# Output projection kept in PSUM under the feed-forward, first up product by token tiles, fewer semaphore clears: layers 2 and 3 of a three-layer block

## The reference

```python
x = x + mixer(rmsnorm(x, norm_mix)) @ w_out          # the output projection
h = rmsnorm(x, norm_ffn)
x = x + (silu(h @ w_gate) * (h @ w_up)) @ w_down     # D_FF = 2816 hidden columns
```

## Time and profile before

| | us |
|---|---|
| timed runs: median of 3 (lowest, highest) | 1140.2 (1139.49, 1145.4) |
| profiled execution, first to last instruction (span) | 1135.1 |
| PE busy in it | 998.4 |
| layer 2, output stage, from its first DMA | 568.08 |
| layer 3, output stage, from its first DMA | 921.86 |
| feed-forward of layer 3, up(0) begins | 952.39 |

### The profile page before, as it was taken

The page is one execution under the profiler, slowest core; times in us unless marked ns, Lnnn a source line. Parts: engine busy times, 40 slices in busy tenths (PEclk is TensorE's granted clock), DMA queues, the critical chain, the costliest instruction groups (busy, mean ns, idle before and its releaser), DMA issues. The chain is left out here.

```text
span 1135.1 us, 20168 instructions
## 1 busy us (share of the span) xinstructions
PE 998.4 (88%) x8497; PEld 710.3 (63%) x8499; DVE 590.4 (52%) x950; ACT 486.3 (43%) x795; POOL 101.3 (9%) x111
## 2 busy tenths in 40 slices
PE   6998899799666677998799999997998879999996
PEld 5675787455333344886547777775885536777773
DVE  5566589421000004688666555435667865555543
ACT  5456452310000004545556455524545656645532
POOL 3410360000000001033000000002040000000000
PEclk9899899799888898998889999998998999999999
DMA  9822005999999996452094755525422046666520
GB/s 273 247 90 82 2 3 226 422 409 420 421 421 421 421 411 195 155 177 76 1 329 133 243 193 184 183 105 153 149 82 75 1 174 216 223 222 204 188 89 37
DMA packets 108324, 228.56 MB, mean 201 GB/s; under 512 B 7145, under 2 KB 86043, under 8 KB 93659
## 3 DMA queue, kind: packets, MB, share of 16 engines
q1 hardware_dynamic: 105275, 219.38, 53.2%
q0 software_dynamic: 2976, 8.14, 2.5%
HBM read 224.63 MB, written 1.05 MB: 199 GB/s over the span
## 5 line engine op out<-in xcount | busy, mean ns | idle before, releaser
L524 DVE SCALAR_TENSOR_TENSOR ffn_wu_lo<-ffn_w_up,ffn_wu_hi 128x2048 f16<-128x2048 f32 x44 | 99.0, 2288 | 55.2 <-ACT ffn_wu_hi L449 55.2
L1132 PE MATMUL rw_pB<-ring,kept 128*32 128x256 f32 x864 | 69.2, 418 | 31.4 <-DMA ring<-in_w_up 22.0
L669 PE MATMUL ffn_pG<-ffn_hT_hi,ffn_wu_hi 128*128 128x256 f16 x352 | 96.0, 273 | 0.3
L669 PE MATMUL ffn_pG<-ffn_hT_lo,ffn_wu_hi 128*128 128x256 f16 x352 | 96.0, 273 | 0.0
L669 PE MATMUL ffn_pG<-ffn_hT_hi,ffn_wu_lo 128*128 128x256 f16 x352 | 96.0, 273 | 0.0
L669 PE MATMUL ffn_pU<-ffn_hT_hi,ffn_wu_hi 128*128 128x256 f16 x352 | 95.9, 273 | 0.0
L669 PE MATMUL ffn_pU<-ffn_hT_hi,ffn_wu_lo 128*128 128x256 f16 x352 | 95.9, 273 | 0.0
L669 PE MATMUL ffn_pU<-ffn_hT_lo,ffn_wu_hi 128*128 128x256 f16 x352 | 95.9, 273 | 0.0
L449 ACT ACTIVATE ffn_wu_hi<-ffn_w_up 128x2048 f16<-128x2048 f32 x44 | 81.7, 1901 | 2.5 <-DMA ffn_w_up<-in_ffn_w_gate 2.3
L1132 PEld LDWEIGHTS rw_pB<-ring,kept 128*32 128x32 f32 x864 | 37.9, 120 | 59.9 <-issue 46.6
L249 DVE SCALAR_TENSOR_TENSOR in_w_lo<-wt,in_w_hi 128x2048 f16<-128x2048 f32 (+2 forms) x22 | 52.7, 2396 | 35.7 <-ACT in_w_hi L242 35.2
(11 more groups left out here) (651 smaller groups left out, 2129.1 us busy)
## 6 DMA issues: line engine op xcount, KB each, us to landing
ring<-in_w_gate SPq DMA_DIRECT2D x27, 1024.0 KB, 26.1
ring<-in_w_up SPq DMA_DIRECT2D x27, 1024.0 KB, 26.4
ring<-in_w_down SPq DMA_DIRECT2D x26, 1024.0 KB, 26.6
ffn_w_up<-in_ffn_w_gate SPq DMA_DIRECT2D x22, 1024.0 KB, 7.6
ffn_w_up<-in_ffn_w_up SPq DMA_DIRECT2D x22, 1024.0 KB, 9.8
ffn_w_down<-in_ffn_w_down SPq DMA_DIRECT2D x22, 1024.0 KB, 5.1
wt<-in_ev_w_in SPq DMA_DIRECT2D x9, 1024.0 KB, 5.6
wt<-in_od_w_in SPq DMA_DIRECT2D x9, 1024.0 KB, 6.4
```

The lines of the kernel that those rows point to most:

```text
L524: return nc.vector.scalar_tensor_tensor(out, whole, scale, hi, ALU.mult, ALU.subtract)
L669: ins = T.matmul(p[:, s, j * SEQ:(j + 1) * SEQ], w[:, s, m, c, j::NJ], h[:, c, :], start=(n == 0), stop=(n == 3 * KC - 1))
L1132: ins = nc.tensor.matmul(into[i * CAP:(i + 1) * CAP, 0:D_EXPERT], h[:, c, i * CAP:(i + 1) * CAP], held[:, c * D_EXPERT:(c + 1) * D_EXPERT] ...
```

## The change

It is made in layers 2 and 3 alone, in three parts.

1. **Semaphores.** A new class `Held` takes the semaphores of all three stages of a layer and clears them once, at the layer's end, with one barrier. The stages in between end with the barrier of their Block only.
2. **Projection sums stay.** `add_out` writes `x` plus projection into `xn`, and leaves `x` and `pY` as they are. The norm works in place on `xn` (the squares go to the `gated` buffer). The down products add to the projection's sums, and the final addition to `x` brings both. `clear`, `add_zeros` and the zero tile are gone.
3. **First up product by token tiles.** `up(0)` becomes `up_first`: for each tile `t`, gate or up `m`, and half `j`, 24 products with 128 tokens, in all 192 instead of 96. Two and a half groups of tile 0 stand ahead of the turning of tile 1, one and a half behind it, then the four groups of tile 1. The turned tiles lie one bank pair per `t`, and are signalled, and waited for, four chunks at a time instead of two.

```diff
+class Held:
+    def take(self, name, names):
+        own = [self.nc.alloc_semaphore(f"{name}_{n}") for n in names]
+        self.sems += own
+        return own
+    def __exit__(self, *exc):
+        if exc[0] is None:
+            self.nc.clear_and_free_semaphores(self.sems)
+            self.nc.all_engine_barrier()
...
-        turned_of = lambda t, c: (pG, pU)[c // 4][:, c // 2 % 2, t * SEQ + c % 2 * P:t * SEQ + (c % 2 + 1) * P]
-        with Stage(nc, name, ["pair2_in", "pair3_in", "gain_in", "wo_hi", "wo_lo", "out_done", "x_added", "x_squares", "x_recips", "x_roots",
+        turned_of = lambda t, c: (pG, pU)[c // 4][:, t, c % 4 * P:(c % 4 + 1) * P]
+        squares = gated[:].rearrange("p s n -> p (s n)")
+        sems = held.take(name, ["pair2_in", "pair3_in", "gain_in", "wo_hi", "wo_lo", "out_done", "x_added", "x_squares", "x_recips", "x_roots",
...
-                            if c % 2 == 0:
-                                act.wait_ge(xn_turned, KC // 2 * t + c // 2 + 1)
+                        if c % 4 == 0:
+                            act.wait_ge(xn_turned, 2 * t + c // 4 + 1)
...
-                        nc.vector.scalar_tensor_tensor(own, pY[:, t, n * 512:(n + 1) * 512], 1.0 / W_SCALE, own, ALU.mult,
+                    nc.vector.scalar_tensor_tensor(xn[:, t, own], pY[:, t, own], 1.0 / W_SCALE, x[:, t, own], ALU.mult,
...
-                            dve.wait_ge(hT_high, t * KC + c // 2 * 2 + 2)
+                        dve.wait_ge(hT_high, t * KC + c // 4 * 4 + 4)
...
-                    nc.vector.memset(zeros[:], 0.0).then_inc(zeroed, 1)
...
+                def up_first(t, m, j, chunks=range(KC)):
+                    own = slice(t * P, (t + 1) * P)
+                    into = (pG, pU)[m][:, 0, j * SEQ + t * P:j * SEQ + (t + 1) * P]
+                    for n, (w, h) in enumerate(((wu_hi, hT_hi), (wu_lo, hT_hi), (wu_hi, hT_lo))):
+                        for c in chunks:
+                            if m == 0 and j == 0 and n != 1:
+                                pe.wait_ge(hT_low if n else hT_high, t * KC + c + 1)
+                            ins = T.matmul(into, w[:, 0, m, c, j::NJ], h[:, c, own], start=(c == 0 and n == 0),
+                                           stop=(c == KC - 1 and n == 2), skip_group_check=True)
+                    return ins
...
-                    pe.wait_ge(zeroed, 1)
-                    for t, n in ((0, 0), (0, 1), (1, 0), (1, 1)):
-                        clear(t, n, 2 * t + n + 1)
-                    add_zeros(8)
-                    turn(1, 4)
-                    add_zeros(3)
-                    up(0, 0, 0, first=True)
+                pe.wait_ge(hT_low, KC)
+                pe.wait_ge(up_lo, 3)
+                up_first(0, 0, 0)
+                up_first(0, 0, 1)
+                up_first(0, 1, 0, range(4))
+                turn(1)
+                up_first(0, 1, 0, range(4, KC))
+                up_first(0, 1, 1)
+                for m in range(2):
+                    for j in range(NJ):
+                        ins = up_first(1, m, j)
+                ins.then_inc(up_done, 1)
```

More of the change, by code:

```diff
@@ L736, in _ @@
-                    last_down(n_blocks - 1, (n_blocks - 1) % 2)
+                                    ins = down_one(s, t, j, half, n, j == NJ - 1 and n == 2)
+                            ins.then_inc(summed, 1)
+                pe.sem_inc(up_done, 2)
+                pe.sem_inc(down_done, 2)
+                for k in range(KC // 2):
+                    pe.wait_ge(wo_high, k + 1)
+                    for term in range(3):
+                        if term == 2:
+                            pe.wait_ge(wo_low, k + 1)
+                        for c in (2 * k, 2 * k + 1):
+                            for n in range(2):
+                                ins = project(0, c, n, term)
@@ new lines, in _ @@
+                ins.then_inc(out_done, 1)
+                for n in range(2):
+                    for c in range(KC):
+                        for term in range(3):
+                            ins = project(1, c, n, term)
+                    ins.then_inc(out_done, 1)
+                    if n == 0:
+                        turn(0)
+                pe.wait_ge(hT_low, KC)
[3 more added lines that the diff above has]
+                up_first(0, 1, 0, range(4))
@@ new lines, in _ @@
+                turn(1)
+                up_first(0, 1, 0, range(4, KC))
+                up_first(0, 1, 1)
+                for m in range(2):
+                    for j in range(NJ):
+                        ins = up_first(1, m, j)
+                ins.then_inc(up_done, 1)
+                with pe.Fori(0, turns) as i:
+                    up(i * 2 + 1, 1, i)
+                    down(i * 2, 0, i)
+                    up(i * 2 + 2, 0, i + 1)
+                    down(i * 2 + 1, 1, i)
+                if n_blocks % 2 == 0:
+                    up(n_blocks - 1, 1, turns)
+                    down(n_blocks - 2, 0, turns)
@@ L2972, in even_attention @@
-def even_attention(nc, con, y, e, low, outT, start):
+        sems = held.take("in2", Projection.NAMES + side)
+        pr.take(sems[:len(Projection.NAMES)])
+        (rows_in, ckv_normed, kr_roped, ik_roped, iq_roped, qr_roped, qb_roped, kb_roped, rel_used, ckv_turned, k_made,
+         v_made, kr_turned, idx_turned, idx_scored, q_turned, qb_turned, kb_turned, ckv_out, k_out, kr_twice, kr_out,
+         v_out, ik_twice, idx_out, related, q_out, qb_out, kb_out, ckv_squared, ckv_rstd, vlink, glink) = sems[len(Projection.NAMES):]
@@ L2974, in even_attention @@
+def even_attention(nc, held, con, y, e, low, outT, start):
     units = 8
@@ L3429, in sparse_attention @@
+def sparse_attention(nc, held, con, y, o, low, outT, start):
     per_group = PAIRS // C_G
```

2079 lines of the change are left out of this document (1019 added, 1060 removed).

## The result

| | before, us | changed, us |
|---|---|---|
| timed runs: median (lowest, highest, number) | 1139.49 (1129.64, 1145.4, 13) | 1145.65 (1137.49, 1149.5, 13) |
| profiled execution: span | 1135.1 | 1145.2 |

The ratio of the times is 1.0058, with a 95% interval of 1.0035 to 1.0081: the change costs 0.6%, where 0.2% was forecast, too little to tell from no change. The measured median lies inside the stated range (1136.5 to 1146.0), near its upper end. The medians are over all executions, the ratios over those within 1.5% of a kernel's fastest, which leaves out a few of the longest. The profiled execution of the changed kernel took 1147.12 us of its own, 1.9 above its span and 1.5 above the median.

A forecast was written before the change was run, and what follows sets the result against it. TensorE, busy 998.4 of 1135.1 us, was taken as the bound, with up(1) also held by VectorE's low halves. 1135.1 - 1.6 + 0.2 + 3.4 = 1137.1 us span, plus 5.1 gives 1142.2; range 1136.5 to 1146.0.

The forecast's parts named there:

- the stall: TensorE idle 4.0 us ahead of up(1), waiting for block 1's low halves; up(1) about 0.1 us later in each layer.
- the handoff of 0.17 us: Before the change, up(1) starts 0.17 us behind the end of block 1's low halves on VectorE.
- dear short products: First up product: 128-column products cost 0.109 us, as much as long ones; 1150.6 us, chance 0.10.
- a split that pays: up(1) not bound by block 1's low halves, starting at 958.92; 9.5 us less, 1130.7 us, chance 0.08.
- The boundaries: Ends of projection and attention stages, layers 2 and 3: 2.4 us saved, 0.8 returned at layer ends, net -1.6.
- the clock at the start of layer 3's attention: A shorter wait ahead might keep the attention start's clock high, saving 1.1 us in each layer; not in the sum.
- The clock after the stall: Behind TensorE's wait ahead of up(1), one short fall of the clock per layer: 1.7 us each, +3.4 together.
- Its own last sentence: Prediction wrong if up(1) starts without waiting, pace exceeds 0.08, or other stages' times move more than the boundaries explain.
- The offset: Timed median taken as 5.1 us above the profiled span, turning 1137.1 us of span into 1142.2.

The follow-up runs named there:

- the early halves: Changed kernel with block 1's gate and up weights split sooner on ScalarE and VectorE, so its low halves end earlier; 1128.89 us, ratio 0.9921.
- four kernels that moved it: Useless products in layer 2: 22 or 31 ahead of up(1), 15 at the end, or 4 with block 1's weights split sooner; ratios 0.9981, 1.003, 1.0032, 0.99.
- the fourth: Changed kernel with useless products ahead of up(1), 22 in layer 2 and 18 in layer 3; 1134.2 us, ratio 0.9981.
- the 15 products at the end: Changed kernel, its wait ahead of up(1) left in, with 15 useless products behind layer 2's last down product; 1140.19 us, ratio 1.0032.

## Why the prediction was wrong

**Right.** The pace of a product with 128 columns was forecast at 0.057 us and is 0.056. By the rule of the Trainium skill ("TensorE: Matmul & The Clock Gate", "Back-to-back issue gap", about 81 ns at 128 columns) the turning would, as an estimate, have come 1.4 us later; the trace does not agree with it. The turning came 3.49 behind the projection (forecast 3.5), the low halves ended 12.47 behind it (12.5), up(1) was 0.1 us late, the stall 4.01 us (4.0). The 0.1 came out by luck: with the handoff of 0.17 us that the prediction names, 962.92 gives 963.09, 0.2 late. The handoff was 0.06 in the changed kernel (971.15 to 971.21), so before it was likely PE's own up(0), not the low halves, that held up(1) for the last 0.1 us. The rivals of dear short products and of a split that pays are refuted by these rows, and the early halves show that the latter needed just what was said against it, VectorE 4 us sooner.

**The boundaries** gave 0.7 us behind layer 2's projection (0.12 from barrier to product instead of 0.83), 0.7 and 0.5 behind layer 3's two stages, 0.5 behind layer 2's attention, 2.4 in all as forecast; the clears of 0.57 and 0.61 us at the layers' ends took back 0.9 (forecast 0.8). The net is -1.5 for the forecast -1.6. What the sum left out, and kept as a bound, is the clock at the start of layer 3's attention, another 2.2 us in the kernel with the clears alone, and 1.5 in the changed kernel, in which that stage still ran at 1.2 GHz for 6.8 us.

**The step that failed** is "The clock after the stall": "I take one short fall in each layer: 1.7 us, +3.4 together". Two things are wrong with it. The smaller: the local falls cost 1.8 and 2.75, so 4.5, inside the bounds given; with the 18 filling products both are gone. The larger: it prices the clock only in the microseconds behind the stall. The change makes layer 2's output stage another 2.6 us longer and moves all behind it, and with that the next stage starts at a distance from the clock's fall (3.2 and 3.0 us in its two profiles, 2.3 before) at which it costs 6.5 us, 37 us into code that the prediction costed at nothing. The sum has no term for it and no rival named it. Its own last sentence did name the sign: "if the time of other stages moves by more than the boundaries explain".

With its terms as the changed kernel's profile has them: 1135.1 - 1.5 + 0.2 + 4.5 + 6.1 = 1144.4 (6.1 is the 6.5 of the table less the clear of layer 2, 0.45, which lies in that stage and is in the 1.5 already). What is left nearly cancels: layer 1 +3.3; beside the boundaries, layer 2's projection -0.9 and attention +0.9, layer 3's attention -1.5; output stages +0.3 and -1.4. Together +0.7, so 1145.1 for the 1145.2 measured. Of the -1.4 in layer 3's output stage most stands at its start, where ScalarE could begin on the third quarter of `w_out` 5.0 us behind the barrier instead of 6.7. Why that quarter landed sooner, by more than the boundary, is open.

**The offset.** "The median of the runs lies 5.1 above the span" took two things for one. An execution lies 1.9 us above its own span (1147.12 to 1145.2, and 1145.31 to 1143.4 in the second profile of it). By that the profiled execution of before took about 1137.0 (an estimate, its own time is not on record), 2.5 below the median of 13, and the median of the first three was another 0.7 above. That the measured time lies in the stated range is luck: with an offset of 1.9 the forecast had been 1139.0 and the range had ended at 1142.8.

**What stays open.** The distance between the stage's start and the clock's fall goes with the outcome in all twelve profiles. Of four kernels that moved it, three gave the stage that was forecast, in both directions; the fourth moved it the other way than meant. These are single executions. Of the timed runs of those three, only the interval of the 15 products at the end (up to 1.006) excludes its rival, 1.008; the other two hold theirs. Why a distance of 3 us brings a fall in the middle of dense work 37 us into the stage, and 2.2 or 4.1 does not, no run shows. That the spread of the times of each kernel (16 us for before) and the two groups of one comes from executions that land on either side is likely, not shown: the profile of the early halves is of the upper group and has the long stage, and no execution of its lower group was profiled.

## What to carry to other kernels

Before an edit shortens one of two things that end together, move the other: here the split was worth nothing alone, and 4.2 us in layer 2 and 1.8 to 3.4 in layer 3 once VectorE's low halves came sooner. Where idle time of TensorE can't be avoided, fill it with products that are overwritten: 18 of them in each layer turned a loss of 0.6% into a gain of 0.25%. Of these 11 us only 4.5 are the clock behind the waits; 6.3 came from where the next stage started, which another kernel need not get. And when a time moves by more than the edited place explains, compare the stages that were not edited, their granted clock first, and run a version that only shifts them: a difference of half a per cent can lie in where the run stands when it reaches the next stage.

## What the hardware showed unexpectedly

- The granted clock fell to 1.2 GHz for 13.6 us while PE was busy in 13.60 of them, in products of 65 and 256 columns, with the last wait (1.00 us) over 2.2 us before. The Trainium skill ("TensorE: Matmul & The Clock Gate", "HAM oscillation — how this bites in real kernels") ties such falls to idle gaps of the engine; the two falls behind the stalls agree, this one does not.
- Whether it happens goes with the start of the stage to within 0.6 us in twelve profiles (2.3 against 2.9), and with 15 useless products of 3.2 us the stage was 6 us shorter.
- The clock's falls lie elsewhere in each execution in layer 1 (first fall at 37.8 and 47.4 us), yet nine of twelve executions have the first fall 2.0 to 2.3 us behind the start of layer 2's output stage.
- Clearing the semaphores of three stages takes POOL 0.57 to 0.61 us, those of one stage 0.13 to 0.74.
